# Hybrid encoder layer on one core: expert weights loaded in 4 MB chunks instead of 2 MB, in a ring of 4 places instead of 8

## The chip, the cores and the metric

The kernel runs on one core of one Trainium2 chip. Its time is device microseconds of one execution. The number to compare is the median of several runs; for the kernel before it is 1094.7 us of three runs (1090.6 to 1095.1). All times on the trace count from the start of the span of one profiled execution.

## What is computed

One encoder layer over 256 tokens of width 1024: a mixer (gated linear attention in four heads beside softmax attention in eight) and then a mixture of experts. The experts matter here. Cut to them:

```python
def moe_ffn(x, w_router, b_router, w1, b1, w2, b2):
    logits = (xt @ w_router + b_router)
    top_val, top_idx = lax.top_k(logits, TOP_K)          # 4 of 32
    gates = jax.nn.softmax(top_val, axis=-1)
    ...
    def expert_block(args):
        h = (xb @ w1[e] + b1[e]).astype(jnp.float32)
        h_glu = jnp.minimum(h[:, :D_FF], SWIGLU_LIMIT)
        h_lin = jnp.clip(h[:, D_FF:], -SWIGLU_LIMIT, SWIGLU_LIMIT)
        act = (h_glu * jax.nn.sigmoid(SWIGLU_ALPHA * h_glu) * (h_lin + 1.0))
        return act @ w2[e] + b2[e]
```

All weights are float32. An expert has a first layer of 1024 x 2048 (8 MB) and a second one of 1024 x 1024 (4 MB), so 32 experts are 384 MB (MB here is 2^20 bytes; the profile's MB is 10^6), each byte of which is read once.

## The kernel before

The program has a front part (norm, input projection, mixer, output projection, router) and then the experts, one after the other, each with up to 64 tokens that chose it; further rounds would serve an expert with more, and the inputs here need none. TensorE keeps a tile of 64 gathered tokens still and streams the weights past it, 512 columns at a time; two such products stand side by side in the two halves of the array.

**Loading.** Every weight comes through the DMA queue of SyncE (SP). A chunk is 2 MB, 16 KB for each of 128 partitions (`SLOT` = 4096 floats). An expert is six chunks: four of the first layer (`W1_CHUNKS`, two of eight row blocks each) and two of the second. They go into a ring of eight places (`SLOTS`), 16 MB in all. During the front part the ring's memory holds other things (the input projection's weights, scratch of the linear attention, the output projection's weights in the last two places), so SP waits for a semaphore before each of the first loads: `pass3`, `mix_ps`, `att_used`, `h_ps` (L329 to L342). Two more chunks, numbers 19 and 20, are loaded ahead into the work area (`EARLY` = 2, `EARLY_AT` = 19), where there is room once the attention is done. These two places are used once. So 20 MB are there or under way when the first expert starts.

After that a chunk is loaded into a place when TensorE has finished the chunk that was there: SP waits on `chunk_used` (L351, L357), which TensorE counts up after the last product with each chunk. Chunks 8 to 18 wait for the chunk eight before them. Chunk 21 and all that follow wait for the chunk ten before them, since 19 and 20 stood elsewhere. TensorE in turn waits on the place's own semaphore (`loaded`, L1332 to L1338).

**One expert on TensorE** (`expert`, from L1340): four bias products (L1274), 64 products with the first layer (L1354, 16 for each chunk), the gather of the next expert's tokens (L1318, 48 small products), four products that add the previous expert's result (L1325 by two output rows, 8 in the trace), the turn of the activated tile (L1370, four 128 x 128 transposes), the turn of the gates (L1379), and 32 products with the second layer (L1388, 16 for each chunk). Beside the gather VectorE and ScalarE compute SwiGLU (L975 to L981, L570); ScalarE copies the turned tile out (L573). In the second expert two products after each first-layer chunk open the output sums (`start_row`, L1305).

Rows of a weight matrix are dealt so that a partition's part of a chunk is contiguous in memory: with r rows for each partition, partition p of chunk c holds rows c·128·r + p·r and on. The gather and the turn of the tile must take every r-th column to match, and so must the gains that are loaded in small pieces into `ffn_pairs` (L302 to L306).

Of the kernel before, what the change touches and what calls it, by code (L numbers as in the profile page):

```python
# [24 lines left out]
ACT = mybir.ActivationFunctionType  # L25
AX = mybir.AxisListType

P = 128
SEQ = 256
TILES = SEQ // P  # L30
D = 1024
KD = D // P
# [8 lines left out]
EXPERTS, TOP_K, FF = 32, 4, 1024  # L41
# [15 lines left out]
CAP = 64  # L57
GROUPS = P // CAP
ROUNDS = SEQ // CAP
FG = FF // GROUPS  # L60
SUB = FG // P
SLOTS = 8
SLOT = 4096
B_ROWS = PARTS * EXPERTS
WORK = 14080
EARLY = 2
EARLY_AT = 19
PEELED = EARLY_AT + EARLY + SLOTS
W1_ROWS = SLOT // (2 * FF)
W2_ROWS = SLOT // D  # L70
W1_CHUNKS = KD // W1_ROWS
W2_CHUNKS = FF // (W2_ROWS * P)
PER_EXPERT = W1_CHUNKS + W2_CHUNKS
UNROLL = 4
PER_BODY = UNROLL * PER_EXPERT
assert PER_BODY % SLOTS == 0 and EXPERTS % UNROLL == 0 and W2_CHUNKS == GROUPS and W2_ROWS == SUB
LOADS_PER_BODY = PER_BODY // SLOTS
TABLE = ROUNDS * EXPERTS + UNROLL
ATT_PAIRS = HEADS // KV_HEADS
# [24 lines left out]
def encoder_layer(nc, x, w_in, w_out, w_router, w1, b1, w2, b2, gate_w, columns, rows, final_g,  # L104
                  c_keep, c_front, later, split, out):
    ctx = ExitStack()
    with ctx:
# [7 lines left out]
        ring = sb("ring", [P, SLOTS * SLOT])  # L115
# [3 lines left out]
        ident, iota, before, ones = (ckeep[:, i * P:(i + 1) * P] for i in range(4))  # L119
# [61 lines left out]
        prob = reuse(2, 2 * SEQ)  # L181
        probT = reuse(2, 2 * SEQ)
        mix = [att01[:, 0, :], att01[:, 1, :], att2[:, 0, :], att2[:, 1, :]]
        scratch = Carve(ring, 5 * SLOT)
        gA, gM, gB, gX = (scratch(4, SEQ) for _ in range(4))
        decayed = Carve(ring, KD * D_IN)
        kk = decayed(4, 7, CHUNK)
        assert decayed.at <= 5 * SLOT
        w_in_sb = ring[:, 0:KD * D_IN].rearrange("p (k n) -> p k n", n=D_IN)

        fin_g = ring[:, 0:D]
        w_out_att = ring[:, 6 * SLOT:7 * SLOT].rearrange("p (k n) -> p k n", n=D)
        w_out_gla = ring[:, 7 * SLOT:8 * SLOT].rearrange("p (k n) -> p k n", n=D)

# [27 lines left out]
        glu = back(FG)  # L224
        lin = back(FG)
        sig = back(FG)
        hidT = back(SUB, P)
        part0 = back(TILES * D // 2).bitcast(BF16).rearrange("p (t d) -> p t d", d=D)
        gateT = back(SEQ)
        res = back(D // GROUPS)  # L230
# [54 lines left out]
        def _(sp):  # L285
# [13 lines left out]
            sp.dma_start(later_sb, later).then_inc(S.const_in, 16)  # L299
            sp.dma_start(wr_sb, w_router.rearrange("p (k e) -> p k e", e=EXPERTS)).then_inc(S.const_in, 16)  # L300
            sp.dma_start(b2_sb, b2).then_inc(S.b2_in, 16)
            for half in range(2):  # L302
                for r in range(W1_ROWS):
                    sp.dma_start(ffn_pairs[half * 64:(half + 1) * 64, r:KD:W1_ROWS],
                                 columns[r:P:W1_ROWS, KD + half:2 * KD:W1_ROWS],
                                 allow_slow_non_contiguous=True).then_inc(S.pairs_in, 16)  # L306

            for kv in range(KV_HEADS):
# [13 lines left out]
            def first_ring(s):  # L322
                load(slot(s), slot_in[s], s // PER_EXPERT, s % PER_EXPERT)
# [2 lines left out]
                load(early[i], early_in[i], (EARLY_AT + i) // PER_EXPERT, (EARLY_AT + i) % PER_EXPERT)  # L326


            for s in range(4):  # L329
                sp.wait_ge(S.pass3, min(KD, ((s + 1) * SLOT - 1) // D_IN + 1))  # L330
                first_ring(s)
            sp.wait_ge(S.pass3, KD)
            sp.wait_ge(S.mix_ps, 2)
            for s in range(4, 6):
                first_ring(s)
            sp.wait_ge(S.attT_ps, ATT_PAIRS)
            for i in range(EARLY):
                load_early(i)
            sp.wait_ge(S.att_used, 1)
            first_ring(6)  # L340
            sp.wait_ge(S.h_ps, TILES)
            first_ring(7)  # L342
            sp.wait_ge(S.extra_done, 1)

            rounds = sp.value_load(extra[0:1, 0:1], min_val=0, max_val=ROUNDS - 1)
# [96 lines left out]
        def _(act):  # L442
# [124 lines left out]
            def expert(n):  # L567

                act.wait_ge(S.glu_ready, n + 1)
                nc.scalar.activation(sig, glu, ACT.Sigmoid, scale=ALPHA).then_inc(S.sig_ready, 1)  # L570

                act.wait_ge(S.hidT_ps, n + 1)
                nc.scalar.activation(hidT, bank[5][:, :].rearrange("p (s q) -> p s q", q=P), ACT.Copy)\  # L573
                    .then_inc(S.hidT_sb, 1)

                act.wait_ge(S.gatedT_ps, n + 1)
                nc.scalar.activation(gatedT, bank[7][:, 0:SEQ].rearrange("p (t q) -> p t q", q=P), ACT.Copy)\
                    .then_inc(S.gatedT_sb, 1)

                act.wait_ge(S.chunk_used, (n + 1) * PER_EXPERT)  # L580
                nc.scalar.activation(res, bank[6][:, :], ACT.Copy).then_inc(S.res_ready, 1)  # L581
# [22 lines left out]
        def _(dve):  # L604
# [381 lines left out]
            dve.wait_ge(S.sel_table, ROUNDS)  # L986
            bias_select(0)
            tables()
            dve.wait_ge(S.pairs_in, 16 * GROUPS * W1_ROWS)
            gathered_out(0)  # L990
            later_rounds()
            dve.wait_ge(S.gateT_ps, 1)
# [39 lines left out]
        def _(pe):  # L1032
# [310 lines left out]
            def expert(n, q, it, first=False, second=False):  # L1343


                start_hidden(n)
                pe.wait_ge(S.xg_ready, n + 1)
                for c in range(W1_CHUNKS):
                    chunk = by_row(loaded(q, c, it), 2 * FF)
                    for r in range(W1_ROWS):  # L1350
                        k = c * W1_ROWS + r
                        for j in range(GROUPS):
                            for g in range(2):
                                last = mm(bank[(2, 5)[g]][j * CAP:(j + 1) * CAP, :], xg[:, k * CAP:(k + 1) * CAP],  # L1354
                                          chunk[:, r, g * FF + j * FG:g * FF + (j + 1) * FG], start=False, stop=k == KD - 1,
                                          skip_group_check=True)
                    last.then_inc(S.chunk_used, 1)

                    if second:
                        start_row(c)  # L1360
                gather(n + 1)
                if not first:
                    pe.wait_ge(S.res_ready, n)
                    for i in range(4):
                        combine(i)

                pe.wait_ge(S.hid_ready, n + 1)
                apart = lin.rearrange("p (m r) -> p m r", r=W2_ROWS)
                for r in range(W2_ROWS):
                    last = nc.tensor.transpose(bank[5][:, r * P:(r + 1) * P], apart[:, :, r], ident)  # L1370
                last.then_inc(S.hidT_ps, 1)

                pe.wait_ge(S.gated_ready, n + 1)
                if first:
                    pe.wait_ge(S.gateT_sb, 1)
                else:
                    pe.wait_ge(S.gatedT_sb, n)
                for t in range(TILES):
                    last = nc.tensor.transpose(bank[7][:, t * P:(t + 1) * P], gated[:, t, :], ident)  # L1379
                last.then_inc(S.gatedT_ps, 1)  # L1380
                pe.wait_ge(S.hidT_sb, n + 1)
                pe.wait_ge(S.xg_ready, n + 2)

                for s in range(W2_CHUNKS):
                    chunk = by_row(loaded(q, W1_CHUNKS + s, it), D)
                    for r in range(W2_ROWS):
                        for j in range(GROUPS):
                            last = mm(bank[6][j * CAP:(j + 1) * CAP, :], hidT[:, r, s * CAP:(s + 1) * CAP],  # L1388
                                      chunk[:, r, j * 512:(j + 1) * 512], start=s == 0 and r == 0,
                                      stop=s == W2_CHUNKS - 1 and r == W2_ROWS - 1, skip_group_check=True)  # L1390
                    last.then_inc(S.chunk_used, 1)
# [63 lines left out]
```

## Time and profile before

| | us |
|---|---|
| median of three runs | 1094.7 |
| lowest, highest | 1090.6, 1095.1 |
| the profiled execution | 1092.3 |
| its span, first to last instruction | 1090.3 |
| TensorE busy with products | 983.2 |
| VectorE busy | 230.1 |
| ScalarE busy | 117.4 |
| expert part, from the first product with expert weights to the last result | 169.3 to about 1080 |

The profile's time lines cut the span into 40 slices of 27.3 us. Its line of the DMA engines says what share of the time the 16 engines were at work, the line under it how many GB/s they moved. The chain of waits follows the program back from its last instruction, each step to what released it. "Granted clock" is the share of its full speed that TensorE was given; 1.00 is its level of 2.4 GHz and 0.50 that of 1.2 GHz. The trace does not name a chunk; which transfer a row shows follows from the order of the queue.

### The profile page before, as it was taken

How to read it: one execution, taken by the hardware profiler on the slowest of the kernel's cores; microseconds unless marked ns; L12 is line 12 of the kernel's file. 1: busy time of each engine (PE TensorE's matmuls, PEld its weight loads, DVE VectorE, ACT ScalarE, POOL GpSimd, SP SyncE). 2: the span in 40 equal slices, each digit the busy share in tenths (PEclk: the TensorE clock that was granted, in tenths of full speed). 3: DMA queues.
4: the chain of work that ended last, by engine and by line, in shares of the span. 5: the costliest groups of instructions: out<-in, count | busy, mean ns of one | idle time of the engine just before them, and what ended most of it. 6: DMA issues, size and time to landing. Idle time of an engine off the chain costs nothing.

```text
span 1090.3 us, 13890 instructions
## 1 busy us (share of the span) xinstructions
PE 983.2 (90%) x5869; PEld 425.6 (39%) x5869; DVE 230.1 (21%) x531; ACT 117.4 (11%) x226; POOL 20.3 (2%) x24
## 2 busy tenths in 40 slices
PE   6997878999999999988889888998988888898885
PEld 4644544344444444433333333333333333333332
DVE  1577344111111111111111001111111111110113
ACT  1053130000000000000000000000000000000002
POOL 0010020000000000000000000000000000000000
PEclk9998998999999999999999999999999999999998
DMA  9924746999999999999999999999999999999993
GB/s 319 287 110 209 308 154 253 429 421 417 394 426 426 429 427 429 429 427 429 429 429 428 429 428 429 428 429 429 429 429 428 429 428 429 428 429 429 429 429 161
DMA packets 33093, 421.31 MB, mean 386 GB/s; under 512 B 4880, under 2 KB 5136, under 8 KB 7376
## 3 DMA queue, kind: packets, MB, share of 16 engines
q1 hardware_dynamic: 33072, 421.02, 92.6%
q8 instruction: 15, 0.25, 0.1%
q14 instruction: 6, 0.05, 0.0%
HBM read 419.95 MB, written 1.05 MB: 386 GB/s over the span
## 4 chain that ended last, share of the span: by engine, by line
PE 49%; DMA 42%; DVE 5%; ACT 2%; issue 1%; POOL 0%; SPq 0%; POOLq 0%; DVEq 0%
DMA ring<-in_w_dram 41%; PE bank L1354 20%; PE bank L1388 12%; PE bank L1057 4%; PE bank L1325 3%; PE bank L1318 3%; PE bank L1265 1%; PE bank L1370 1%; ACT work L573 1%; PE bank L1253 1%; PE bank L1274 1%; DMA h<-in_x_dram 1%; ACT work L522 1%; PE bank L1198 0%; PE bank L1143 0%
## 5 line engine op out<-in xcount | busy, mean ns | idle before, releaser
L1354 PE MATMUL bank<-ring,work 128*64 128x512 f32 x2016 | 458.0, 598 | 51.2 <-DMA ring<-in_w_dram 50.0
L1354 PEld LDWEIGHTS bank<-ring,work 128*64 128x64 f32 x2016 | 166.6, 136 | 324.2 <-issue 210.7
L1388 PE MATMUL bank<-ring,work 128*64 128x512 f32 x1024 | 226.8, 595 | 15.5 <-ACT work L573 15.5
L975 DVE TENSOR_SCALAR work<-bank 128x512 f32<-128x512 f32 x32 | 22.1, 692 | 726.9 <-PE bank L1354 726.9
L1388 PEld LDWEIGHTS bank<-ring,work 128*64 128x64 f32 x1024 | 71.2, 137 | 150.5 <-issue 132.9
L570 ACT ACTIVATE work<-work 128x512 f32<-128x512 f32 x32 | 20.2, 632 | 539.1 <-DVE work L975 539.1
L1325 PE MATMUL bank<-work 64*128 64x512 f32 x256 | 63.6, 615 | 0.7 <-ACT work L581 0.7
L1318 PE MATMUL bank<-work,tok 128*128 128x64 bf16 x1056 | 50.8, 194 | 0.0
L1318 PE MATMUL bank<-work 128*128 128x64 bf16 x528 | 49.0, 195 | 1.2 <-DVE work L948 1.2
L1318 PEld LDWEIGHTS bank<-work,tok 128*128 128x128 bf16 x1056 | 47.4, 99 | 0.0
L1318 PEld LDWEIGHTS bank<-work 128*128 128x128 bf16 x528 | 33.7, 99 | 27.2 <-issue 27.2
L581 ACT ACTIVATE work<-bank 128x512 f32<-128x512 f32 x32 | 19.1, 597 | 221.7 <-PE bank L1388 221.7
L1325 PEld LDWEIGHTS bank<-work 64*128 64x128 f32 x256 | 22.0, 186 | 18.2 <-issue 15.1
L573 ACT ACTIVATE work<-bank 128x512 f32<-128x512 f32 x32 | 19.1, 597 | 88.4 <-PE bank L1370 88.4
L393 POOL TENSOR_TENSOR stat<-stat 128x1 f32<-128x1 f32 (+2 forms) x8 | 9.4, 1178 | 1019.5 <-DVE stat L614 1019.5
L1370 PEld LDWEIGHTS bank<-ckeep,work 128*128 128x128 f32 x128 | 17.8, 208 | 24.9 <-DVE work L981 24.2
L968 DVE TENSOR_SCALAR work<-ckeep,work 128x128 f32<-128x128 f32 x64 | 19.3, 344 | 30.0 <-PE bank L1379 30.0
L1370 PE MATMUL bank<-ckeep,work 128*128 128x128 f32 x128 | 23.9, 309 | 1.3 <-DVE work L981 1.3
L960 DVE TENSOR_TENSOR work<-bank,ffn_pairs 128x512 f32<-128x512 f32 x33 | 22.5, 682 | 0.7 <-PE bank L1318 0.7
L981 DVE TENSOR_TENSOR work<-work 128x512 f32<-128x512 f32 x32 | 22.1, 692 | 1.1
L978 DVE SCALAR_TENSOR_TENSOR work<-work 128x512 f32<-128x512 f32 x32 | 22.1, 692 | 1.1
L1057 PE MATMUL bank<-ring,work 128*128 128x512 f32 (+1 forms) x64 | 21.9, 486 | 0.0
(190 smaller groups left out, 487.8 us busy)
## 6 DMA issues: line engine op xcount, KB each, us to landing
ring<-in_w_dram SPq DMA_DIRECT2D x190, 2048.0 KB, 33.1
ring<-in_w_in_dram SPq DMA_DIRECT2D x8, 1168.0 KB, 18.7
work<-in_w_dram SPq DMA_DIRECT2D x2, 2048.0 KB, 12.0
ring<-in_w_out_dram SPq DMA_DIRECT2D x2, 1024.0 KB, 14.5
ring<-in_w_out_dram SPq DMA_DIRECT2D x1, 2048.0 KB, 21.1
h<-in_x_dram SPq DMA_DIRECT2D x2, 512.0 KB, 4.7
out_dram<-tok SPq DMA_DIRECT2D x4, 256.0 KB, 2.4
tok<-in_b_dram SPq DMA_DIRECT2D x3, 256.0 KB, 16.6
```

The lines of the kernel that those rows point to most:

```text
L570: nc.scalar.activation(sig, glu, ACT.Sigmoid, scale=ALPHA).then_inc(S.sig_ready, 1)
L573: nc.scalar.activation(hidT, bank[5][:, :].rearrange("p (s q) -> p s q", q=P), ACT.Copy)\
L960: nc.vector.tensor_tensor(xg.rearrange("p (k c) -> p k c", c=CAP), bank[6][:, :].rearrange("p (k c) -> p k c", c=CAP), ffn_pairs.rearrange ...
L975: nc.vector.tensor_scalar(glu, bank[2][:, :], LIMIT, None, ALU.min).then_inc(S.glu_ready, 1)
L978: nc.vector.scalar_tensor_tensor(lin, lin, 1.0, glu, ALU.add, ALU.mult).then_inc(S.dve_step, 1)
L981: nc.vector.tensor_tensor(lin, lin, sig, ALU.mult).then_inc(S.hid_ready, 1)
L1057: return mm(o, l, r, start=a and first, stop=z, skip_group_check=True)
L1318: last = mm(bank[6][:, k * CAP:(k + 1) * CAP], piece, onehot[:, t, :], start=i == 0 and t == 0, stop=i == PARTS - 1 and t == TILES - 1)
L1325: last = mm(bank[Y[i]][:, :], gatedT[j * CAP:(j + 1) * CAP, t, :], res[j * CAP:(j + 1) * CAP, :], start=False, stop=stop, skip_group_check ...
L1354: last = mm(bank[(2, 5)[g]][j * CAP:(j + 1) * CAP, :], xg[:, k * CAP:(k + 1) * CAP], chunk[:, r, g * FF + j * FG:g * FF + (j + 1) * FG], s ...
L1370: last = nc.tensor.transpose(bank[5][:, r * P:(r + 1) * P], apart[:, :, r], ident)
L1388: last = mm(bank[6][j * CAP:(j + 1) * CAP, :], hidT[:, r, s * CAP:(s + 1) * CAP], chunk[:, r, j * 512:(j + 1) * 512], start=s == 0 and r == 0,
```

## The change

A chunk is 4 MB with 32 KB for each partition. An expert is three chunks: two halves of the first layer (four row blocks each) and the whole second layer. The ring has four places of twice the size, in the same memory. One early place of 4 MB takes the memory of the two (chunk 10, the same weights as 20 and 21 before).

```diff
-SLOTS = 8
-SLOT = 4096
+SLOTS = 4
+SLOT = 8192
-EARLY = 2
-EARLY_AT = 19
+EARLY = 1
+EARLY_AT = 10
...
-            for half in range(2):
+            for u in range(W1_ROWS):
                 for r in range(W1_ROWS):
-                    sp.dma_start(ffn_pairs[half * 64:(half + 1) * 64, r:KD:W1_ROWS],
-                                 columns[r:P:W1_ROWS, KD + half:2 * KD:W1_ROWS],
+                    sp.dma_start(ffn_pairs[u * P // W1_ROWS:(u + 1) * P // W1_ROWS, r:KD:W1_ROWS],
+                                 columns[r:P:W1_ROWS, KD + u:2 * KD:W1_ROWS],
...
-            for s in range(4):
+            for s in range(2):
                 sp.wait_ge(S.pass3, min(KD, ((s + 1) * SLOT - 1) // D_IN + 1))
                 first_ring(s)
-            sp.wait_ge(S.pass3, KD)
+            sp.wait_ge(S.kk_done, 1)
             sp.wait_ge(S.mix_ps, 2)
-            for s in range(4, 6):
-                first_ring(s)
+            first_ring(2)
             sp.wait_ge(S.attT_ps, ATT_PAIRS)
             for i in range(EARLY):
                 load_early(i)
             sp.wait_ge(S.att_used, 1)
-            first_ring(6)
             sp.wait_ge(S.h_ps, TILES)
-            first_ring(7)
+            first_ring(3)
...
                     if second:
-                        start_row(c)
+                        start_row(2 * c)
+                        start_row(2 * c + 1)
...
                 for r in range(W2_ROWS):
-                    last = nc.tensor.transpose(bank[5][:, r * P:(r + 1) * P], apart[:, :, r], ident)
+                    for j in range(GROUPS):
+                        half = slice(j * CAP, (j + 1) * CAP)
+                        last = mm(bank[5][half, r * CAP:(r + 1) * CAP], apart[:, :, r], ident[:, half], start=True, stop=True)
...
-                            last = mm(bank[6][j * CAP:(j + 1) * CAP, :], hidT[:, r, s * CAP:(s + 1) * CAP],
+                            last = mm(bank[6][j * CAP:(j + 1) * CAP, :], hidT[:, r, :],
```

`W1_ROWS` goes from 2 to 4 and `W2_ROWS` from 4 to 8 with `SLOT`. The four transposes of the activated tile become sixteen products with one half of the identity each, which place the two halves of the hidden units one under the other. The small loads into `ffn_pairs` become sixteen of 32 x 2 values instead of four of 64 x 4.

The queue of SP from the loads of the front part on, before. `ring` and `work` are the places, `in_w` the expert weights (L317 first layer, L320 second), and the brackets name the semaphores waited for:

```order
L317 DMA ring<-in_w_dram 128x4096 [waits pass3] x4
L320 DMA ring<-in_w_dram 128x4096 [waits mix_ps,pass3]
L320 DMA ring<-in_w_dram 128x4096
L317 DMA work<-in_w_dram 128x4096 [waits attT_ps]
L317 DMA work<-in_w_dram 128x4096
L317 DMA ring<-in_w_dram 128x4096 [waits att_used]
L317 DMA ring<-in_w_dram 128x4096 [waits h_ps]
L345 TENSOR_LOAD extra [waits extra_done]
L345 ISA x2
L317 DMA ring<-in_w_dram 128x4096 [waits chunk_used] x2
L320 DMA ring<-in_w_dram 128x4096 [waits chunk_used] x2
```

And the same queue with the change:

```order
L317 DMA ring<-in_w_dram 128x8192 [waits pass3] x2
L320 DMA ring<-in_w_dram 128x8192 [waits mix_ps,kk_done]
L317 DMA work<-in_w_dram 128x8192 [waits attT_ps]
L317 DMA ring<-in_w_dram 128x8192 [waits h_ps,att_used]
L343 TENSOR_LOAD extra [waits extra_done]
L343 ISA x2
L317 DMA ring<-in_w_dram 128x8192 [waits chunk_used]
L320 DMA ring<-in_w_dram 128x8192 [waits chunk_used]
```

Each load is twice the size; the load that stood alone after `att_used` has joined the one after `h_ps`, and each wait on `chunk_used` now stands before 4 MB.

TensorE at the end of the first expert before (turn of the tile, turn of the gates, second layer; `slot_in4` and `slot_in5` are the places' semaphores):

```order
L1370 MATMUL bank<-ckeep,work 128x128 [waits hid_ready]
L1370 MATMUL bank<-ckeep,work 128x128 x3
L1379 MATMUL bank<-ckeep,work 128x128 [waits gateT_sb,gated_ready]
L1379 MATMUL bank<-ckeep,work 128x128
L1388 MATMUL bank<-ring,work 64x512 [waits slot_in4,xg_ready,hidT_sb]
L1388 MATMUL bank<-ring,work 64x512 x7
L1388 MATMUL bank<-ring,work 64x512 [waits slot_in5]
L1388 MATMUL bank<-ring,work 64x512 x7
```

And with the change:

```order
L1371 MATMUL bank<-ckeep,work 64x64 [waits hid_ready]
L1371 MATMUL bank<-ckeep,work 64x64 x15
L1380 MATMUL bank<-ckeep,work 128x128 [waits gateT_sb,gated_ready]
L1380 MATMUL bank<-ckeep,work 128x128
L1389 MATMUL bank<-ring,work 64x512 [waits slot_in2,xg_ready,hidT_sb]
L1389 MATMUL bank<-ring,work 64x512 x15
```

The listing counts row blocks by 8 products before and 16 now, where the trace shows the two halves of the array apart (16 and 32). One wait for a landed chunk stands before the whole second layer, and the turn is sixteen small products.

## Rows read from the trace of the kernel before

**Rows 1.** The page: granted clock, DMA share, GB/s by slice; the chain of waits.

```profile
PEclk9998998999999999999999999999999999999998
DMA  9924746999999999999999999999999999999993
GB/s 319 287 110 209 308 154 253 429 421 417 394 426 426 429 427 429 429 427 429 429 429 428 429 428 429 428 429 429 429 429 428 429 428 429 428 429 429 429 429 161
...
PE 49%; DMA 42%; DVE 5%; ACT 2%; issue 1%; POOL 0%; SPq 0%; POOLq 0%; DVEq 0%
```

**Rows 2.** TensorE by time: one expert while no chunk is awaited (start, us).

```profile
252.07 13.79 PE bank L1354 x64
265.86 1.51 PE bank L1318 x48
267.37 1.92 PE bank L1325 x8
269.29 0.69 PE bank L1370 x4
...
270.65 7.09 PE bank L1388 x32
...
278.17 13.79 PE bank L1354 x64
```

**Rows 3.** Stretches: time, busy PE, PEld, DVE, ACT, POOL, clock, DMA, GB/s.

```profile
461.00:1060.00 599.00, 539.19 (x3290) 212.59 (x3288) 87.20 (x200) 42.48 (x81) 0.00 (x0) 1.00 1.01 429
```

**Rows 4.** TensorE's timeline around 500 us, with the wait for the chunk.

```profile
499.10 3.70 PE L1354 MATMUL bank<-ring,work 128*64 128x512 f32 x16 [1.19 <-DMA ring<-in_w_dram]
504.00 3.70 PE L1354 MATMUL bank<-ring,work 128*64 128x512 f32 x16 [1.20 <-DMA ring<-in_w_dram]
```

**Rows 5.** SP's queue by time: weight loads as they are issued.

```profile
15.91 19.00 SPq L304 DMA_DIRECT2D ffn_pairs<-in_columns_dram  x4
...
73.75 11.72 SPq L317 DMA_DIRECT2D ring<-in_w_dram  x4
```

**Rows 6.** SP's queue from 255 us: a load issued when expert 3 is half through its second layer.

```profile
255.59 10.90 SPq L320 DMA_DIRECT2D ring<-in_w_dram  x2
274.54 11.04 SPq L317 DMA_DIRECT2D ring<-in_w_dram  x4
```

**Rows 7.** The same stretches view, around that load.

```profile
274.00:276.00 2.00, 2.00 (x12) 0.72 (x10) 0.00 (x0) 0.00 (x0) 0.00 (x0) 1.00 0.67 147
276.00:278.00 2.00, 2.00 (x14) 0.66 (x9) 0.00 (x0) 0.22 (x1) 0.00 (x0) 1.00 0.68 262
```

**Rows 8.** DMA packets of 461 to 1056 us, nearly all of 16 KB.

```profile
DMA packets 17511, 254.98 MB, mean 429 GB/s; under 512 B 1949, under 2 KB 1949, under 8 KB 1949
```

**Rows 9.** DMA packets of 8 to 14 us: `w_in`, 9344 bytes for a partition.

```profile
DMA packets 305, 2.55 MB, mean 425 GB/s; under 512 B 32, under 2 KB 32, under 8 KB 32
```

**Rows 10.** DMA packets of 52 to 54 us: `w_out`, pieces of 4096 bytes.

```profile
DMA packets 197, 0.81 MB, mean 403 GB/s; under 512 B 0, under 2 KB 0, under 8 KB 197
```

**Rows 11.** The chain of waits through the last expert.

```profile
1061.92 3.71 PE bank L1354 x16
1065.62 1.51 PE bank L1318 x48
1067.13 1.92 PE bank L1325 x8
...
1070.41 7.11 PE bank L1388 x32
1077.53 0.02 issue
```

**Rows 12.** TensorE's timeline, small float32 products of the mixer at full clock.

```profile
108.27 1.99 PE L1191 MATMUL bank<-ring 64*64 64x64 f32 x30
```

**Rows 13.** The chain of waits: first product with `w_out`; small products of the router.

```profile
129.19 7.13 PE bank L1253 x16
...
152.49 1.70 PE bank L1242 x16
```

**Rows 14.** TensorE's timeline before and in a stretch of lower clock.

```profile
112.24 1.09 PE L1133 MATMUL bank<-ckeep,work 128*128 128x128 f32 x8 [1.69 <-DVE work L793]
114.46 1.77 PE L1143 MATMUL bank<-work 128*64 128x256 f32 x8 [1.12 <-DVE work L814]
```

**Rows 15.** Stretches: two at the lower clock, before the experts.

```profile
95.00:100.00 5.00, 5.00 (x55) 3.89 (x56) 2.55 (x7) 3.00 (x10) 0.00 (x0) 0.50 0.03 10
115.00:120.00 5.00, 5.00 (x30) 3.57 (x26) 0.69 (x1) 1.08 (x2) 0.00 (x0) 0.69 1.03 439
```

More of the change, by code:

```diff
@@ L75 @@
 PER_BODY = UNROLL * PER_EXPERT
-assert PER_BODY % SLOTS == 0 and EXPERTS % UNROLL == 0 and W2_CHUNKS == GROUPS and W2_ROWS == SUB
+assert PER_BODY % SLOTS == 0 and EXPERTS % UNROLL == 0
 LOADS_PER_BODY = PER_BODY // SLOTS
@@ L183, in encoder_layer @@
         mix = [att01[:, 0, :], att01[:, 1, :], att2[:, 0, :], att2[:, 1, :]]
-        scratch = Carve(ring, 5 * SLOT)
+        scratch = Carve(ring, 5 * SLOT // 2)
         gA, gM, gB, gX = (scratch(4, SEQ) for _ in range(4))
@@ L187, in encoder_layer @@
         kk = decayed(4, 7, CHUNK)
-        assert decayed.at <= 5 * SLOT
+        assert decayed.at <= 5 * SLOT // 2
         w_in_sb = ring[:, 0:KD * D_IN].rearrange("p (k n) -> p k n", n=D_IN)
         fin_g = ring[:, 0:D]
-        w_out_att = ring[:, 6 * SLOT:7 * SLOT].rearrange("p (k n) -> p k n", n=D)
-        w_out_gla = ring[:, 7 * SLOT:8 * SLOT].rearrange("p (k n) -> p k n", n=D)
+        w_out_att = ring[:, 6 * SLOT // 2:7 * SLOT // 2].rearrange("p (k n) -> p k n", n=D)
+        w_out_gla = ring[:, 7 * SLOT // 2:8 * SLOT // 2].rearrange("p (k n) -> p k n", n=D)
         early = [work[:, KD * SEQ + i * SLOT:KD * SEQ + (i + 1) * SLOT] for i in range(EARLY)]
@@ L226, in encoder_layer @@
         sig = back(FG)
-        hidT = back(SUB, P)
+        hidT = back(W2_ROWS, CAP)
         part0 = back(TILES * D // 2).bitcast(BF16).rearrange("p (t d) -> p t d", d=D)
@@ L572, in expert @@
                 act.wait_ge(S.hidT_ps, n + 1)
-                nc.scalar.activation(hidT, bank[5][:, :].rearrange("p (s q) -> p s q", q=P), ACT.Copy)\
+                nc.scalar.activation(hidT, bank[5][:, :].rearrange("p (s q) -> p s q", q=CAP), ACT.Copy)\
                     .then_inc(S.hidT_sb, 1)
@@ L988, in _ @@
             tables()
-            dve.wait_ge(S.pairs_in, 16 * GROUPS * W1_ROWS)
+            dve.wait_ge(S.pairs_in, 16 * W1_ROWS * W1_ROWS)
             gathered_out(0)
```

## Prediction

> **What bounds the kernel now.** I read the page first [rows 1]. TensorE is busy 90% of the span, yet the chain of waits gives it only 49% and the DMA engines 42%. The slices say where: from the eighth on the DMA engines are always busy at 426 to 429 GB/s, apart from the two slices of 394 and 417. Then I read the expert part in two halves.
>
> Up to about 461 us TensorE never waits for a weight. An expert costs it 278.17 - 252.07 = 26.1 us: 13.79 for the first layer, 1.51 + 1.92 for gather and combine, the turn and its copy, 7.09 for the second layer [rows 2]. The DMA engines need 12.58 MB / 429 GB/s = 29.3 us for the same expert, so TensorE eats up the 20 MB that were loaded ahead and then waits, 1.2 us before a 2 MB chunk [rows 4], with its clock at 1.00 and the DMA engines at 1.01 of their time [rows 3]. From there to the end the weight stream sets the pace. So the end is: when the stream begins to run without a break, plus its bytes, plus what TensorE does after the last bytes.
>
> When does that stream begin? Not at the first expert. While expert 3 uses chunks 19 and 20, which stood in the early places, no load is released, and the queue runs dry: 147 and 262 GB/s between 274 and 278 us [rows 7]. It starts again when SP issues the next load at 274.54 [rows 6], which waited for the first half of expert 3's second layer (270.65 + 7.09/2 = 274.2) [rows 2]. Everything before this point is set by TensorE, everything after it by the DMA engines. The 27 chunks ahead of it in the stream carry no weight in the sum.
>
> **The change, step by step.** The sum is made against the profiled execution, 1092.3 us with a span of 1090.3; the median of the runs is 1094.7, 2.4 above it.
>
> 1. *The pinned load.* It now holds both halves and waits for the whole second layer of expert 3: 7.09/2 = +3.5 us. The first experts also each do the new turn (step 4), four of them before this point: +1.2. What is awaited there is in both kernels TensorE's own progress, so that the very first refill also waits for 32 products instead of 16 costs nothing more: by my schedule from [rows 2] and a 4 MB transfer of 9.8 us the load before the pinned one lands some 3 us before TensorE releases it. Together **+4.7**.
>
> 2. *The stream.* After that point 80 chunks of 4 MB follow, each eight rows of 32 KB on each of the 16 engines instead of sixteen of 16 KB. What does a row cost beyond its bytes? Three stretches with the engines fully busy: 4096-byte rows go at 403 GB/s, 9344 at 425, 16384 at 254.98 MB / 595 us = 428.5 [rows 8 to 10]. Per row and engine that is 162.6, 351.8 and 611.7 ns. Continued from the last two, a 32 KB row takes 1216.6 ns; from the first and the last 1210.5. Against 2 x 611.7 = 1223.4 it saves 6.8 to 12.9 ns, times 80 x 8 rows = 4.4 to 8.3 us. The 403 comes from 2 us of trace, so neither slope is sure; I take the middle, **-6.3**.
>
> 3. *The tail.* Before, the last half of a first layer lands and TensorE starts on it at 1061.92; 15.6 us later the second layer is done at 1077.53 [rows 11]. Two chunks of 4.9 us land in between, so that is 5.8 us after the last landing. Now 32 products follow the last first-layer chunk: 7.2 instead of 3.7, then the same 4.8 to the second layer and 7.1 for it, 19.1 us in all, of which 9.7 lie before the last landing. That leaves 9.4: **+3.6**. The chunk has landed 2.3 us before the second layer starts, so this layer does not wait for it; the price comes from the larger first-layer chunk.
>
> 4. *The turn.* Four transposes take 0.69 us [rows 2]. Sixteen products of 64 x 64 float32: 30 of that form took 1.99 us [rows 12], 66 ns each, so 1.06: +0.3. Bounds: zero, since the same 512 columns of PSUM are written and two halves of the array can work side by side; and +1.0, by sixteen products of a similar size that took 1.70 [rows 13]. I take 0.3, since the form is the same. It counts four times in step 1 and once in the tail, **+0.3** (bounds for all five: 0 to +5).
>
> 5. *At no cost.* The sixteen small loads for `ffn_pairs` move as many values. SP needed 19.0 us for four of them, most of it queueing, and is next wanted at 73.75 [rows 5]; the `w_out` loads behind them are used at 129.19 [rows 13]. Even 20 us more on SP would be covered. The first weight load now waits for four steps of `pass3` instead of two, and 2 MB move from `att_used` to `h_ps`; nothing is wanted of them before 169 us. That the gather takes every fourth column instead of every second costs nothing by [rows 2]: the turn, which takes every fourth column, costs 0.69 for four, as the plain turn of the gates would.
>
> 6. *The ring.* Three chunks ahead instead of seven, the same bytes. In the stretch that the stream bounds a place is released at most about 10 us after its chunk landed, and the queue runs dry only after 29. No cost.
>
> Sum: 4.7 - 6.3 + 3.6 + 0.3 = +2.3, so 1094.6 for an execution like the profiled one, and about **1097** for the median.
>
> The Trainium skill has a rule that speaks against step 2 ("DMA: Bandwidth & Descriptors", Why small descriptors are slow): a fixed overhead of about 3 cycles for a packet, worth removing only at 256 bytes or less. At the fabric's 850 MHz of the same page this is an estimate of 3.5 ns a row, 2.3 us over the stream, and the sum would be +6.3. The three rates of this trace ask for two to four times that.
>
> **Rivals.** *A: rows bring little or nothing.* The transfer may still be cut into 16 KB packets, or the fixed share of a row may be far below what two short stretches suggest. Then the saving is 0 to 2 us and the sum +6.6 to +8.6, 1101 to 1103.5: slower by 0.6 to 0.8%. For it: no packet above 16 KB exists in this trace, and the long stretch is within 1% of the 425 of rows half as long. Against it: every row so far was one packet, whatever its length, up to 16 KB. It decides the sign as soon as less than about 3 us of step 2 are left.
>
> *B: TensorE loses clock in longer waits.* The wait is now 9.7 less 7.4 (32 products and the bias ahead of them), 2.3 us, before the second first-layer chunk, where it was 1.2. Ahead of the stretch at a share of 0.69 [rows 15] stood waits of 1.69 and 1.12 us with little between them [rows 14]; eight products then took 1.77 instead of about 1.1 us. The stream isn't touched: TensorE has 3.2 us to spare per expert, and once it is late there is no long wait. But the last expert pays: a share of 0.69 over 5 us is 3.1 us at the lower level, a loss of 1.6 us; the other stretch is at 0.50 for its whole 5 us [rows 15], and twice that would cost 5. Sum +4 to +7.3, 1099 to 1102.
>
> *C: faster.* With the larger saving of step 2 and a turn that costs nothing the sum is 3.5 - 8.3 + 3.6 = -1.2. For a gain of 5.5 us the saving would have to be 12.6 us, 19.7 ns for a 32 KB row, and so a rate of 435.6 GB/s, 1.7% above what the long stretch has [rows 8]. Nothing in the rows reaches that for long; the sum would be 1089.2. The Trainium skill ("DMA: Bandwidth & Descriptors", Where 436 GB/s comes from) puts the ceiling of the fabric at 435.2 GB/s; by that C can't happen through the rate alone, and the 429 here lies under it.
>
> *D: the ring is too coarse.* If a release came over 29 us after the landing, the engines would idle in every expert, 1 us each being +20 us in all. By [rows 2] the longest path from a landing to its release is 4.8 + 7.1 less the head start, 10 us. I give it little.
>
> **How the numbers follow.** Forecast with its own bounds (saving 4.4 to 8.3, turn 0 to 5): -1.2 to +8, that is 1093.5 to 1102.5 with 1097 in the middle, chance 0.56, of which 0.46 within 0.5%. A 0.17, slower. B 0.14, half of it beyond 0.5%. C 0.10, half of it beyond. D 0.03. 0.5% is 5.5 us, about what a measurement of this kernel can tell from no change, since three runs of it lie 4.5 us apart. So faster 0.05, same 0.58, slower 0.37. The range takes in the forecast, A, most of B, and below it the near half of C: 1091 to 1104.
>
> **What would show it.** In the profile after: GB/s in the long stretch (431 to 433 if step 2 is right, 429 if A is), and half as many packets there; the load after the early place issued about 4.7 us later than 274.5; TensorE's wait before a first-layer chunk 2 to 2.5 us, once an expert; the end of the second layer 19.4 us after the start on the last first-layer chunk; the granted clock in the second half still 1.00, or a share below it if B is right; sixteen turns in about 1.06 us. It would be wrong if the stream ran dry elsewhere, if the expert's 26.1 us grew by more than 3, or if 32 KB rows were slower than 16 KB ones, which no row here can exclude.

## The result

| | before | after |
|---|---|---|
| median of nine runs, us | 1091.4 | 1098.7 |
| lowest, highest | 1090.2, 1095.1 | 1097.2, 1101.1 |
| profiled execution, its span | 1092.3, 1090.3 | 1101.1, 1099.3 |
| TensorE busy | 983.2 | 1028.5 |
| DMA packets | 33093 | 19462 |

The changed kernel takes 1.0057 times as long, 95% interval 1.0036 to 1.0077. The 1098.7 lies in the predicted range of 1091 to 1104 and 1.7 us above the 1097. Against 1092 us the ratio is +6.2 us (the two medians are 7.3 apart), where the sum said +2.3. The nearness of the two times comes in good part from their base: the 1097 was built on 1094.7, a median of three runs, and nine runs gave 1091.4. The ratio also lies just over the 0.5% within which the prediction called a kernel the same, with an interval that reaches below it. So the size needs a closer look. Two terms of the sum were right, the turn was far off, and some costs were not in it.

The page after, the lines that answer to [rows 1]:

```profile
PEclk9998988999999999999999999999999999999998
DMA  9925735999799999999999999999999999999991
GB/s 324 286 77 231 306 153 242 405 385 437 322 427 434 429 430 435 429 433 433 430 434 429 432 434 429 432 435 429 433 433 430 434 429 433 434 428 432 435 430 78
...
PE 63%; DMA 28%; DVE 5%; ACT 2%; issue 1%; POOL 0%; SPq 0%; POOLq 0%; DVEq 0%
```

From the twelfth slice on the stream is as fast as before or faster, but the eleventh has 322 GB/s where it had 394: the queue ran dry for longer. Now the long stretch and its packets, to be held against [rows 3, 8] (time, busy time of PE, PEld, DVE, ACT and POOL, clock, DMA share, GB/s; then the packets of 461 to 1056 us):

```profile
461.00:1060.00 599.00, 570.59 (x3952) 260.00 (x3950) 91.55 (x210) 44.16 (x84) 0.00 (x0) 1.00 1.00 432
```

```profile
DMA packets 8828, 256.94 MB, mean 432 GB/s; under 512 B 987, under 2 KB 987, under 8 KB 987
```

Half as many packets carry more bytes. And TensorE is busy 571 us of these 599, not 539.

Where TensorE's time went shows in the chain of waits through expert 3 (start and length in us), against [rows 2]:

```profile
256.97 13.79 PE bank L1352 x64
270.75 1.72 PE bank L1316 x48
272.47 1.92 PE bank L1323 x8
274.39 2.10 PE bank L1371 x32
...
277.16 7.09 PE bank L1389 x32
...
284.25 0.43 PE bank L1272 x4
```

The turn takes 2.10 us and has 32 rows; it took 0.69 with four. The gather takes 1.7 instead of 1.51. SP's queue shows the pinned load 10.0 us later than in [rows 6], and the DMA engines had nothing at all to do before it (the view of stretches):

```profile
284.52 0.35 SPq L317 DMA_DIRECT2D ring<-in_w_dram  x1
```

```profile
280.00:285.00 5.00, 5.00 (x27) 1.76 (x25) 0.00 (x0) 0.60 (x1) 0.00 (x0) 1.00 0.00 0
```

The last expert in the chain of waits, against [rows 11]:

```profile
1066.64 7.14 PE bank L1352 x32
1073.77 1.69 PE bank L1316 x48
1075.46 1.92 PE bank L1323 x8
1077.38 2.10 PE bank L1371 x32
...
1080.15 7.11 PE bank L1389 x32
1087.26 0.02 issue
```

It begins on the last first-layer chunk 4.7 us later than before (1066.64 against 1061.92) and needs 20.6 us instead of 15.6. So the path is: pinned load +10.0; a larger first transfer into the empty queue and then 79 faster ones, together -5.3; last expert +5.0. That is +9.7 at the end of the second layer, and +9.0 for the span, as what follows was 0.7 shorter. This execution is the slowest of the nine, 2.4 us above their median, so its +9 is more than the +6.2 of the ratio.

### The profile page after: what moved, and what is told of

Read it like the earlier page. It is cut to its first block, busy times and chain, and to the rows that moved or that the text cites. A ratio compares the mean times of both kernels' runs of the same rounds, so it can differ in the third digit from the quotient of the medians.

```text
span 1099.3 us, 15373 instructions
## 1 busy us (share of the span) xinstructions
PE 1028.5 (94%) x6765; PEld 489.6 (45%) x6765; DVE 230.1 (21%) x531; ACT 117.4 (11%) x226; POOL 20.3 (2%) x24
## 2 busy tenths in 40 slices
DMA packets 19462, 421.33 MB, mean 383 GB/s; under 512 B 3536, under 2 KB 3792, under 8 KB 6032
## 4 chain that ended last, share of the span: by engine, by line
PE 63%; DMA 28%; DVE 5%; ACT 2%; issue 1%; POOL 0%; SPq 0%; POOLq 0%; DVEq 0%
PE bank L1352 28%; DMA ring<-in_w_dram 27%; PE bank L1389 14%; PE bank L1371 4%; PE bank L1055 4%; PE bank L1323 4%; PE bank L1316 3%; PE bank L1263 1%; ACT work L571 1%; PE bank L1272 1%; PE bank L1251 1%; DMA h<-in_x_dram 1%; ACT work L520 1%; PE bank L1141 0%; PE bank L1131 0%
## 5 line engine op out<-in xcount | busy, mean ns | idle before, releaser
L1352 PE MATMUL bank<-ring,work 128*64 128x512 f32 x2016 | 445.2, 594 | 22.2 <-DMA ring<-in_w_dram 22.2
L1352 PEld LDWEIGHTS bank<-ring,work 128*64 128x64 f32 x2016 | 176.4, 136 | 272.9 <-issue 227.2
L1389 PE MATMUL bank<-ring,work 128*64 128x512 f32 x1024 | 228.4, 599 | 11.2 <-ACT work L571 11.2
L1389 PEld LDWEIGHTS bank<-ring,work 128*64 128x64 f32 x1024 | 71.6, 138 | 147.5 <-issue 133.2
L1371 PEld LDWEIGHTS bank<-ckeep,work 128*64 128x64 f32 x1024 | 64.4, 216 | 24.8 <-DVE work L979 24.0
L1371 PE MATMUL bank<-ckeep,work 128*64 128x64 f32 x1024 | 68.8, 287 | 1.2 <-DVE work L979 1.2
L1316 PE MATMUL bank<-work,tok 128*128 128x64 bf16 x1056 | 55.6, 198 | 0.0
L1316 PE MATMUL bank<-work 128*128 128x64 bf16 x528 | 54.0, 199 | 1.2 <-DVE work L946 1.2
L1316 PEld LDWEIGHTS bank<-work,tok 128*128 128x128 bf16 x1056 | 52.7, 116 | 0.0
L1316 PEld LDWEIGHTS bank<-work 128*128 128x128 bf16 x528 | 39.1, 116 | 27.2 <-issue 27.2
## 6 DMA issues: line engine op xcount, KB each, us to landing
work<-in_w_dram SPq DMA_DIRECT2D x1, 4096.0 KB, 14.5
```

The source lines that it names most:

```text
L1316: last = mm(bank[6][:, k * CAP:(k + 1) * CAP], piece, onehot[:, t, :], start=i == 0 and t == 0, stop=i == PARTS - 1 and t == TILES - 1)
L1371: last = mm(bank[5][half, r * CAP:(r + 1) * CAP], apart[:, :, r], ident[:, half], start=True, stop=True)
L1389: last = mm(bank[6][j * CAP:(j + 1) * CAP, :], hidT[:, r, :], chunk[:, r, j * 512:(j + 1) * 512], start=s == 0 and r == 0, stop=s == W2_CH ...
```

## The experiments

Each kernel was timed in the same rounds as the kernel before. Times in us against the kernel before are the ratio's difference from 1, times 1092. The theory that follows from this trace: what TensorE does ahead of the pinned load moves the whole stream; each term that lies there counts fully, and each in the last expert counts once more; the turn lies in both; the saving comes from the longer rows.

### The turn without its cost

`e6_interleaved` deals the hidden units to the two halves of the array by parity, so that four transposes are enough again:

```diff
-                                          chunk[:, r, g * FF + j * FG:g * FF + (j + 1) * FG], start=False, ...
+                                          chunk[:, r, g * FF + j:(g + 1) * FF:GROUPS], start=False, ...
...
-                    for j in range(GROUPS):
-                        half = slice(j * CAP, (j + 1) * CAP)
-                        last = mm(bank[5][half, r * CAP:(r + 1) * CAP], apart[:, :, r], ident[:, half], start=True, stop=True)
+                    last = nc.tensor.transpose(bank[5][:, r * P:(r + 1) * P], apart[:, :, r], ident)
```

> The changed kernel with 32 KB rows and 4 MB chunks kept, but the hidden units dealt to the two halves of the array by parity instead of by lower and upper half: the first-layer products and the bias products read every second column, and the turn of the activated tile is again four transposes of 128 x 128. Nothing is left out. My theory: the sixteen products of the turn are 32 passes of 66 ns, 2.11 us instead of 0.69, and they count five times (four experts before the pinned load, one in the tail): removing them gives back 5 x 1.42 = 7.1 us, so the kernel comes out at about 0 to +2 us against the kernel before, where the changed kernel stands at +7.3. The stretch between gather-and-combine and the copy is again 0.69 us. Rival 1 (the chunk size alone costs, the turn is hidden): it stays at +6 to +7. Rival 2 (reading every second column slows the first-layer products): they take over 13.8 us for an expert and the time gets worse than that of the changed kernel.

Measured: 1.0020 (1.0002 to 1.0038), +2.2 us, so 4.0 less than the changed kernel. Its chain of waits in expert 3:

```profile
252.60 14.51 PE bank L1352 x64
267.11 1.67 PE bank L1316 x48
268.78 1.92 PE bank L1323 x8
270.70 0.69 PE bank L1369 x4
```

The turn is 0.69 again, and rival 1 is out. Part of what it gave back went into the first layer: 14.5 us where contiguous columns take 13.79, so rival 2 is there in small. Reading every second column costs 0.7 us an expert. Five turns give back 7.1 us and five slower first layers take 3.6 of it, so 3.5 should be left, and 4.0 came.

### Rows or transfers

`e2_rows16` keeps the 4 MB transfer and cuts each partition's part into two 16 KB pieces. The turn is the four transposes of before, without another column order for the first layer.

```diff
-                sp.dma_start(to, w1[e].rearrange("(c p r) n -> c p (r n)", p=P, r=W1_ROWS)[r]).then_inc(loaded, 16)
+                sp.dma_start(to.rearrange("p (b n) -> p b n", b=W1_BLOCKS),
+                             w1[e].rearrange("(c b p r) n -> c p b (r n)", b=W1_BLOCKS, p=P, r=W1_ROWS)[r]).then_inc(loaded, 16)
...
-                sp.dma_start(to, w2[e].rearrange("(s p r) n -> s p (r n)", p=P, r=W2_ROWS)[s]).then_inc(loaded, 16)
+                sp.dma_start(to.rearrange("p (b n) -> p b n", b=W2_BLOCKS),
+                             w2[e].rearrange("(b p r) n -> p b (r n)", p=P, r=W2_ROWS)).then_inc(loaded, 16)
```

> Ring of four places and 4 MB transfers as in the changed kernel, but each partition's 32 KB are two pieces of 16 KB from two places of the weight matrix, laid out as before; so the gather, the gains and the turn (four transposes) are those of the kernel before. Nothing is left out. My theory: the saving in the stream comes from longer rows, not from fewer transfers, so the stream goes at 429 GB/s again, 9.78 us for 4 MB, and only the costs of the larger chunk remain: +3.5 at the pinned load, +3.4 in the tail, less 0.8 because the output sums are opened between two chunks and not four: about +6 us against the kernel before. Rival (the saving belongs to the transfer, by its completion, whatever its rows): 9.71 us for 4 MB, 432 GB/s, and the kernel at about 0.

Measured: 1.0082 (1.0052 to 1.0113), +9.0 us. Its packets of 461 to 1056 us:

```profile
DMA packets 16536, 254.94 MB, mean 428 GB/s; under 512 B 976, under 2 KB 976, under 8 KB 976
```

As many transfers as in the changed kernel, and the bytes of before (254.94 MB against 254.98 of [rows 8] and 256.94). The saving belongs to the row. The stream says the same: the pinned load is issued at 278.68, +4.1, and the work with the last first-layer chunk starts at 1065.94, +4.0, so nothing was gained in between, where the changed kernel gained 5.3. The last expert takes 19.0 us, +3.4. The time is 3 us above what the theory gave, with an interval of +5.7 to +12.3 that just holds it. The profiled execution is 1099.1, +6.8 against that of before. The other five runs lie up to 5 us higher, and no trace shows them. A fall of the clock, as in the next section, costs 1.5 to 1.7 us where it lies on the path, so it would take more than one; that was not shown for these runs.

### One part of each

`e3_w2rows16` has 32 KB rows for the first layer; the second layer is loaded and turned as in `e2_rows16`.

```diff
-W2_ROWS = SLOT // D
+W2_ROWS = 4
+W2_BLOCKS = SLOT // (D * W2_ROWS)
...
```

> The changed kernel with 32 KB rows for the first layer, but the second layer as one 4 MB transfer of two 16 KB pieces for each partition, laid out as before, with the four transposes of before. Nothing is left out. My theory: two thirds of the saving of the rows stay (3.9 of 5.9 us; an expert's three transfers take 2 x 9.71 + 9.78 = 29.2 us), the chunk costs of +6 stay, the gather with every fourth column costs 0.17 us five times, and the turn costs nothing: about +3 us against the kernel before. Rival 1 (the turn doesn't matter): +6 to +8, as the changed kernel. Rival 2 (the saving belongs to the transfer): about +1.

Measured: 1.0011 (0.9994 to 1.0027), +1.2 us. It can't be told from the kernel before, and lies 5 us under the changed one: the turn counts. It is also below the +3 of the theory and at the +1 of rival 2, but the trace is against that rival: an expert's three transfers take 29.21 us (507.93 - 478.72 below), which is 2 x 9.71 + 9.79, while the changed kernel, with 32 KB rows everywhere, has 29.14 (571.27 - 542.13 further down). Where the other 2 us are I can't say: the profiled execution is the slowest of the twelve. The trace shows something else (TensorE's timeline, with the wait for the chunk in brackets):

```profile
478.72 8.83 PE L1355 MATMUL bank<-ring,work 128*64 128x512 f32 x32 [2.57 <-DMA ring<-in_w_dram]
507.93 7.14 PE L1355 MATMUL bank<-ring,work 128*64 128x512 f32 x32 [0.99 <-DMA ring<-in_w_dram]
537.15 8.79 PE L1355 MATMUL bank<-ring,work 128*64 128x512 f32 x32 [2.51 <-DMA ring<-in_w_dram]
```

After a wait of 2.5 us the same work with a chunk mostly takes 8.8 us and not 7.14; being late, TensorE waits only 1.0 us for the next expert's chunk and is fast again. Of the twelve waits of 2.5 us after 461 us ten end so; after the two at 654.04 and 858.6 the work takes 7.14. That is rival B of the prediction. The last expert of this execution had it too, and so paid 1.5 us (the stretch there is at the lower level, 0.50):

```profile
1063.00:1066.00 3.00, 2.95 (x8) 1.02 (x9) 0.00 (x0) 0.00 (x0) 0.00 (x0) 0.50 1.03 437
```

The changed kernel itself has no fall after 461 us. Its long turn leaves TensorE only 1.1 to 1.2 us to wait, once an expert:

```profile
542.13 7.14 PE L1352 MATMUL bank<-ring,work 128*64 128x512 f32 x32 [1.15 <-DMA ring<-in_w_dram]
571.27 7.14 PE L1352 MATMUL bank<-ring,work 128*64 128x512 f32 x32 [1.12 <-DMA ring<-in_w_dram]
```

### Twice the turn, in the first four experts only

`e7_turn_twice_first4` is the changed kernel with one line changed; `n` is a plain number in the first four experts alone.

```diff
-                for r in range(W2_ROWS):
+                for r in list(range(W2_ROWS)) * (2 if isinstance(n, int) else 1):
```

> The changed kernel with the sixteen products of the turn done twice (the same results written again) in the first four experts only; the other 28 are untouched. My theory: everything TensorE does before the pinned load moves the whole stream and the end with it, so four times 2.1 us: 8.4 us more than the changed kernel, +15 to +16 against the kernel before, and the load after the early place is issued 8.4 us later. Rival (the stream is the bound from its first refill on and hides what TensorE does in the first experts, and only the last expert's turn counts): no more than 1 us over the changed kernel.

Measured: 1.0114 (1.0086 to 1.0141), +12.4 us, 6.2 more than the changed kernel. SP's queue:

```profile
290.73 0.35 SPq L317 DMA_DIRECT2D ring<-in_w_dram  x1
```

The pinned load is issued 6.2 us later than in the changed kernel's trace, and the end is 6.2 us later by the ratios and 5.9 by the two profiled spans (1105.2 against 1099.3). Work that ends 800 us before the kernel does moves its end by all or nearly all of its time. The rival is out. The size was expected at 8.4: the second set costs 1.93, not 2.1 (7.7 in all), and in the changed kernel's trace a fall of the clock in expert 0 had cost 1.66, which this trace doesn't have.

### A later pause

If the pause after the early places is a cost of both kernels, moving it must help both. `e4_before_early22` moves it in the kernel before:

```diff
-EARLY_AT = 19
+EARLY_AT = 22
```

> The kernel before with one number changed: the two early places hold chunks 22 and 23 (the second layer of expert 3) instead of 19 and 20. Nothing is left out. My theory of what sets the end: the weight stream runs dry while TensorE uses the early places, because nothing is released then, and restarts at TensorE's pace; the later that pause comes, the more of the queue is still unfinished and covers it. By the schedule of the trace before, the load after the pause is issued at about 281.6 us while the one ahead of it lands only at about 283.5, so the pause vanishes and the whole stream ends 3 us earlier: -3 us against the kernel before, with no stretch under 420 GB/s between 270 and 290 us. Rival (the pause is covered by later slack, or the end is set by the first refill and TensorE's start): no change, within 0.5 us.

Measured: 0.9983 (0.9963 to 1.0003), -1.9 us. In the changed kernel (`e8_after_early11`):

```diff
-EARLY_AT = 10
+EARLY_AT = 11
```

> The changed kernel with the early place holding chunk 11 (the second layer of expert 3) instead of chunk 10. Nothing is left out. My theory: the load after the pause waits for the first first-layer chunk of expert 4, released at about 291.6 us, while the ten loads ahead of it end at about 290.7; the break shrinks from 5 us to under 2, and chunk after chunk lands 2.6 us earlier than in the changed kernel: +4.5 to +5 against the kernel before. Rival (the cost of the larger chunks lies wholly in the tail and in the turn): no change against the changed kernel, +7.

Measured: 1.0031 (1.0012 to 1.0050), +3.4 us, 2.8 less than the changed kernel. The theory said 2.6. The two intervals overlap, so the traces must carry it: the work with the last first-layer chunk starts at 1063.11, where the changed kernel had 1066.64. That is 3.5 us, of which 1.3 belong to an expert 4 that began earlier (283.35 against 284.68) and 2.2 to the moved pause. It did not vanish: between 288 and 290 us the DMA engines moved nothing. For the kernel before the theory said 3 and 1.9 came, with an interval that touches no change. The trace of `e4_before_early22` shows a reason: the load after the pause was issued at 283.53 and not at 281.6, since TensorE was 1.6 us late from expert 0 on by a fall of the clock. So a short pause was left, in one stretch:

```profile
282.00:284.00 2.00, 2.00 (x12) 0.82 (x10) 0.00 (x0) 0.00 (x0) 0.00 (x0) 1.00 1.01 418
284.00:286.00 2.00, 2.00 (x12) 0.81 (x10) 0.00 (x0) 0.00 (x0) 0.00 (x0) 1.00 0.89 221
```

### Both, and the clock

`e9_w2rows16_early11` is `e3_w2rows16` with the early place at chunk 11:

> First-layer chunks in 32 KB rows, the second layer as 4 MB of 16 KB rows with the four transposes of before, and the early place holding chunk 11. Nothing is left out. My theory: the same kernel with the early place at chunk 10 came to +2 us; the later pause takes 2.5 us off, so -0.5 to 0 against the kernel before. Rival: +2 as without the move.

Measured: 0.9989 (0.9969 to 1.0008), -1.2 us; 2.4 less than without the move, near the 2.5 expected, though the two intervals overlap. Then the same with work for TensorE inside the long wait:

```diff
                     last.then_inc(S.chunk_used, 1)
+                    if c == 0 and not isinstance(n, int):
+                        pe.wait_ge(S.gatedT_sb, n)
+                        for _ in range(8):
+                            nc.tensor.transpose(bank[7][:, 2 * P:3 * P], ones, ident)
```

> The previous kernel with eight transposes of constants (1.4 us on TensorE, into a part of a bank that nobody reads) after the first of the two first-layer chunks of experts 4 to 31, where TensorE would wait some 2.2 us for the next chunk. Nothing is left out. Theory of the clock: in the kernels with 4 MB chunks and a short turn the granted clock falls to 0.50 for a moment every few experts, because TensorE waits 2.2 us in one piece; with the filler the wait is 0.8 us, the clock stays at 1.00 after 461 us, and the last expert's 32 products after the last first-layer chunk always take 7.14 us (8.66 where the clock had fallen): about 1 us faster than without the filler, -1 to -1.5 against the kernel before. Rival (the falls are not tied to the wait): they go on, and the time is the same or worse by the filler's own delays.

Measured: 0.9992 (0.9972 to 1.0012), -0.9 us: no gain, and the expected 1 us is missed. The clock did what was expected: its mean over the span is 0.983 to 0.987 in all twelve runs, where the twelve without the filler have 0.969 to 0.971. The last expert without the filler, and with it:

```profile
1057.05 8.84 PE L1355 MATMUL bank<-ring,work 128*64 128x512 f32 x32 [2.57 <-DMA ring<-in_w_dram]
```

```profile
1056.94 1.09 PE L1362 MATMUL bank<-ckeep 128*128 128x128 f32 x8
1059.59 7.14 PE L1355 MATMUL bank<-ring,work 128*64 128x512 f32 x32 [1.55 <-DMA ring<-in_w_dram]
```

With the filler the clock reads 1.00 over the whole stretch from 461 to 1060 us, and the work with the chunk takes 7.14. But in this execution the chunk was 2.5 us later to begin with. The filler adds 1.1 us to every expert from the fifth on, also to those in which TensorE sets the pace and the loads wait for it. Of the 2.5 us 0.6 were there before the first filler (expert 4 begins at 277.23 against 276.59), and between 300 and 340 us 16.97 MB were moved where it had been 17.28, another 0.7. The rest I did not separate. No version here is faster than the kernel before by more than its interval; `e4_before_early22` and `e9_w2rows16_early11` come nearest.

## Why the prediction came out as it did

*What bounds the kernel* held. The pinned load was the right place to look: `e7_turn_twice_first4` moved it by intent and the end with it beyond the noise, and the experiments with a later pause point the same way. Three readings around it were wrong, and no number of the sum rests on them. 30 chunks are loaded ahead of the pinned one, not 27. The rule that a chunk waits for the one ten before it ends with chunk 28; from chunk 29 on it is again the one eight before, which is why the pinned chunk 30 waits for chunk 22, the first half of expert 3's second layer. And the ninth slice has 421 GB/s, which is outside the 426 to 429 too.

*Step 1, the pinned load: +4.7 predicted, +10.0 in the trace.* The half chunk gave the 3.5 that was said. The four turns gave 4 x 1.41 = 5.6, not 1.2. Three things were not in the sum: four gathers of 0.17 more (0.7); a fall of the clock in expert 0, whose second layer took 8.75 us instead of 7.09 (+1.7, in this execution); and, on the other side, 0.8 less for the opening of the output sums and 0.7 since the experts began earlier. So the half chunk was sized right, and most of the miss comes in through step 4.

*Step 2, the stream: -6.3 predicted.* 4 MB take 4.194 MB / (256.94 MB / 595 us) = 9.71 us, where [rows 8] give 9.79; over 80 chunks that is 6.0 us. A 32 KB row takes 1214 ns, between the two continuations of 1210.5 and 1216.6. It saves 9 ns. The path got 5.3 of these 6.0; I put the rest down to the larger first transfer into the empty queue, which no run took apart. The rule of the Trainium skill that was set against it ("DMA: Bandwidth & Descriptors", Why small descriptors are slow) would have given 3.5 ns by the prediction's estimate; the trace does not agree, it shows 9 ns between one row of 32 KB and two of 16 KB. Of rival A, the packet count rules out that the transfer is cut at 16 KB, and the 9 ns that longer rows bring nothing.

*Step 3, the tail: +3.6 predicted.* The work with the last first-layer chunk takes 7.14 instead of 3.71, +3.4. Right.

*Step 4, the turn: +0.3 predicted, +1.4 measured, five times.* This is the mistake, and it was in the rows. I took sixteen products at 66 ns. But a float32 product leaves two records in this trace, and a transpose leaves one: 16 products stand as x32 in the turn above, 4 transposes as x4 in [rows 2]. The 66 ns of [rows 12] are for a record: the 30 rows there belong to 16 products of the code (8 places for each of two heads, the other two rows stand apart). Counted so, the very same row gives 32 x 66 = 2.1 us, which is what was measured. The sentence in the part on the change that lays the difference between listing and trace to the halves of the array is wrong for the same reason: the listing counts products, the trace records. (The four bias products of L1272 use both halves too, but are bf16, and leave four.) The 64 and 32 products with the two layers are records as well, 32 and 16 in the code. The upper bound of 1.0 us more was too low too, as it came from counting the router's records as products. Five times 1.1 us are 5.5 us. With them the sum of +2.3 reaches +7.8; the clock in expert 0 (+1.7), the gathers (+0.9), the smaller saving of the stream (+1.0), the tail (-0.2) and the two gains of step 1 (-1.5) bring it to the +9.7 of the trace.

*Step 5.* That a wider column step costs the gather nothing was wrong. It was judged from float32 turns, and the gather is bf16 (groups by line of the page after; `PEld` is the loading of the operand that stays in the array):

```profile
L1316 PEld LDWEIGHTS bank<-work,tok 128*128 128x128 bf16 x1056 | 52.7, 116 | 0.0
L1316 PEld LDWEIGHTS bank<-work 128*128 128x128 bf16 x528 | 39.1, 116 | 27.2 <-issue 27.2
```

Before, these loads took 99 ns each, and in `e2_rows16`, which keeps every second column in 4 MB chunks, they take 99 again. That makes 0.17 us an expert, 0.9 us on the path. The small loads, the queue of SP and the front part were covered, as said.

*Rivals.* B, the clock, was priced right (1.6 us for the last expert; 1.5 to 1.7 measured) and put in the wrong kernel. The falls came in the kernels that wait 2.5 us, as the cheap turn of my sum would have; the dear turn filled that wait to 1.2. C needed a turn that costs nothing. D never showed: in the long stretch the DMA engines are at 1.00 of their time. That 1098.7 lies within the range, and near 1097, is in part luck: the base was 3.3 us too high, and the range was wide enough for a turn that cost more than its own upper bound.

## What to carry over

Find the last moment at which the queue of a stream runs dry: what TensorE did ahead of it moved the end by nearly all of its time, 800 us off, and the longer turn in the 27 experts between it and the last one did not, since the queue never ran dry there. Before pricing an instruction by a row, count on a line of known code how many records one instruction leaves; transposes and products differ. What saved time here was the longer row, not the larger transfer. What a larger chunk costs is half a chunk's compute wherever someone waits for a whole one: here at the pause and at the end.

## What the hardware showed

- Row length still counts at 16 KB: 32 KB rows go at 431.8 GB/s, 16 KB rows at 428.5 (256.94 and 254.98 MB in 595 us). For the 16 KB rows it made no difference whether the transfer was 2 or 4 MB (254.98 and 254.94 MB). Each 32 KB row went as one packet (8828 packets, 987 of them small).
- In `e3_w2rows16` TensorE waited 2.5 us for a chunk and was then, ten times of twelve, at its lower level, 1.2 GHz (granted 0.50), for some us: 8.8 us for a chunk's 32 records instead of 7.14. In `e6_interleaved`, with 17 waits of 1.8 to 1.9 us, this came four times. The kernel before waits 1.2 us at a time and stays at 2.4 GHz [rows 3, 4], and so does the changed one.
- The products with 512 moving float32 columns take 14.5 us for 64 records when they read every second column, 13.79 when the columns are contiguous.
- A bf16 load of 128 columns takes 116 ns with every fourth column and 99 with every second.
- A float32 product leaves two records in the trace, a float32 transpose and a bf16 product one. Turning the same 64 x 1024 values takes 2.10 us as sixteen products and 0.69 us as four transposes.
